# The inverse roots of a head pair's vector lengths: worked out on 88 rows of 12 columns, moved there and back by DMA

## What is computed

```python
def l2_normalize(x):
    xf = x.astype(jnp.float32)
    return xf * lax.rsqrt(jnp.sum(jnp.square(xf), axis=-1, keepdims=True) + EPS)

q = l2_normalize(q.reshape(bsz, t, GDN_HEADS, GDN_DK)) * (GDN_DK ** -0.5)
k = l2_normalize(k.reshape(bsz, t, GDN_HEADS, GDN_DK))
...
y = rms_norm(o, gdn_norm) * jax.nn.silu(zf)
```

## Time and profile before

| | |
|---|---|
| median of 3 runs | 1422.48 us (1421.45 to 1423.62) |
| the profiled execution | 1424.37 us, of which its span is 1422.6 us |
| busy: PE, DVE, ACT | 98%, 71%, 60% of the span |
| mean granted TensorE clock | 0.992 |
| DMA | 180 MB, 127 GB/s on the mean |

### The profile page before, as it was taken

How to read it: one execution, slowest core, us unless ns; L and a number is a source line. 1 busy time by engine, 2 the same in 40 slices (tenths; PEclk the granted TensorE clock), 3 DMA queues, 4 the chain that set the end, 5 groups by cost and what they waited for, 6 DMA issues and landing times.

```text
span 1422.6 us, 30023 instructions
## 1 busy us (share of the span) xinstructions
PE 1387.7 (98%) x9428; PEld 1172.2 (82%) x9428; DVE 1015.9 (71%) x3674; ACT 858.1 (60%) x2780; POOL 290.1 (20%) x339
## 2 busy tenths in 40 slices
PE   9999999999999999999999999999999999999998
PEld 7877887877778777778677787778778999999998
DVE  5767667787777787878778777878665667777543
ACT  5445688686666776666865667666784453444332
POOL 3012222222322222322322312222241000000000
PEclk9999999999999999999999999999999999999999
DMA  9443327644456443375444473434644565555551
GB/s 279 125 118 58 85 50 149 164 104 74 94 119 150 112 107 76 82 170 119 90 98 91 110 141 83 79 76 111 172 91 161 163 238 175 179 178 177 177 179 60
DMA packets 282890, 180.05 MB, mean 127 GB/s; under 512 B 183072, under 2 KB 229696, under 8 KB 282728
## 3 DMA queue, kind: packets, MB, share of 16 engines
q1 hardware_dynamic: 282418, 177.86, 49.4%
q10 hardware_dynamic: 318, 0.33, 0.1%
HBM read 134.32 MB, written 6.77 MB: 99 GB/s over the span
## 4 chain that ended last, share of the span: by engine, by line
PE 81%; DVE 8%; ACT 6%; issue 2%; SPq 1%; DMA 1%; POOL 0%; DVEq 0%; ACTq 0%
PE ps L2067 13%; PE ps L2069 12%; PE ps L2068 12%; PE ps L2471 6%; PE ps L2472 6%; PE ps L2473 6%; ACT ksq L895 2%; PE ps L2142 2%; PE ps L2089 2%; PE ps L2419 2%; PE ps L2143 2%; PE ps L2144 2%; PE ps L2420 2%; PE ps L2421 2%; PE ps L1951 2%
## 5 line engine op out<-in xcount | busy, mean ns | idle before, releaser
L2067 PE MATMUL ps<-ukh,cTh 128*128 128x512 f32 x1024 | 418.1, 408 | 5.5 <-DVE sparts L1285 4.6
L895 ACT ACTIVATE ksq<-ps 128x128 f32<-128x128 f32 x1024 | 268.2, 277 | 252.2 <-PE ps L2069 251.6
L2068 PE MATMUL ps<-ukl,cTh 128*128 128x512 f32 x1024 | 402.6, 393 | 0.0
L2069 PE MATMUL ps<-ukh,cTl 128*128 128x512 f32 x1024 | 402.5, 393 | 0.0
L1285 DVE CUSTOM_DVE_ANT_0 prod<-ps,qb 128x128 f32<-128x128 f32 x1024 | 234.5, 286 | 27.6 <-ACT ksq L895 23.3
L2067 PEld LDWEIGHTS ps<-ukh,cTh 128*128 128x128 f32 x1024 | 194.4, 190 | 60.0 <-issue 22.6
L2069 PEld LDWEIGHTS ps<-ukh,cTl 128*128 128x128 f32 x1024 | 193.9, 189 | 43.0
L2068 PEld LDWEIGHTS ps<-ukl,cTh 128*128 128x128 f32 x1024 | 194.4, 190 | 34.4
L747 POOL TENSOR_TENSOR rk<-kss,mhalf 128x8 f32<-128x8 f32 x128 | 218.4, 1706 | 10.6
L895 ACT ACTIVATION_READ_ACCUMULATOR ksq<-ps 128x1 f32 x1024 | 212.4, 208 | 0.0
L882 ACT ACTIVATE cTr<-turned 128x1024 uint16<-128x1024 uint16 x126 | 174.7, 1386 | 2.7 <-DMA turned<-planes 2.7
(11 more groups left out here) (504 smaller groups left out, 2702.1 us busy)
## 6 DMA issues: line engine op xcount, KB each, us to landing
clat<-cache_mla SPq DMA_DIRECT2D x128, 256.0 KB, 2.6
wraw<-w_in SPq DMA_DIRECT2D x16, 1024.0 KB, 5.2
wraw<-w_up SPq DMA_DIRECT2D x16, 1024.0 KB, 5.4
wraw<-w_down SPq DMA_DIRECT2D x16, 1024.0 KB, 5.0
braw<-w_in SPq DMA_DIRECT2D x24, 512.0 KB, 4.5
crope<-cache_mla SPq DMA_DIRECT2D x128, 32.0 KB, 2.4
qb<-scratch SPq DMA_DIRECT2D x16, 256.0 KB, 3.7
sst<-state_gdn SPq DMA_DIRECT2D x32, 128.0 KB, 3.5
```

What stands on the lines that cost most here:

```text
L895: i = nc.scalar.activation(ksq[m % 3], ps[:, k % 3, P * h:P * h + P], ACT.Square, accum_out=kss[:, n // 4 % 2, n % 4, h0 + h:h0 + h + 1]). ...
L2067: mm(out, cTh[:, n % 2, c], ukh[:, c, cols], start=c == 0, stop=False)
L2068: mm(out, cTh[:, n % 2, c], ukl[:, c, cols], start=False, stop=False)
L2069: i = mm(out, cTl[:, n % 2, c], ukh[:, c, cols], start=False, stop=c == 3)
```

## The change

- The sums of squares of a pair's four rows go to four rows of one group instead of four groups of 32 (L2166: one accumulation over shifted windows of a constant, `start` at the first and `stop` at the last), and DVE reads 4 rows of 264. In the same way the outputs' two rows.
- SP lays each of these rows out on 22 rows of 12 columns (`compact`: one DMA in SBUF for each row, four for the lengths, two for the outputs). Root, reciprocal and Newton step then work on 88 (or 44) rows of 12 columns, in the tile `lc`; the split is gone. The constant column that holds the queries' factor has it on the first 44 rows instead of 64.
- SP writes the result to DRAM (`roots_out`), waits for it, and reads it back on all 128 partitions (`roots_back`, 4 x 264 or 2 x 264 columns). The products that spread the rows (24 calls of `spread_row` in all, with two products each) are gone. DVE scales two heads with one instruction, from SBUF.
- `STEPS`: after step 16 come `ROOT`, `ROOT_OUT`, `ROOT_BACK` and one empty slot before 17; steps 45 and 46 are gone. A pair has 50 slots. The outputs' Newton step, transfers and scaling are done in slots 0, 1, 2 and 14 of the next pair (slot 5 after the last pair), and the first two loads of the next phase, `z_load(0)` and `z_load(1)`, move from slot 232 to slot 241.
- ACT's root of the lengths moves from step 15 to the end of step 16, behind a wait for the four `compact` DMAs, and that of the outputs from step 43 to 44, behind a wait for two.

```diff
-ROOT = 47
-STEPS = list(range(14)) + [None, 14, 15, 16, ROOT] + list(range(17, 47))
+ROOT, ROOT_OUT, ROOT_BACK = 47, 48, 49
+STEPS = list(range(14)) + [None, 14, 15, 16, ROOT, ROOT_OUT, ROOT_BACK, None] + list(range(17, 45))
...
+def tail_slot(i):
+
+    b, p = divmod(i - B_START, B_SLOTS)
+    return (b - 1, p) if 1 <= b <= HP else (None, None)
+
+
+def scale_slot(b):
+    return 14 if b + 1 < HP else 5
...
+            def compact(name, n_):
+                sp.wait_ge(S("a_read"), a_count(name))
+                for c in range(n_):
+                    sp.dma_start(lc[22 * c:22 * c + 22, 0, :], lr[c:c + 1, :].rearrange("c (a b) -> c a b", b=12)).then_inc(S("compacted"), 16)
+
+            def roots_out(b, c0, n_):
+                sp.wait_ge(S("root_ready"), 2 * b + 1 + c0 // 4)
+                sp.dma_start(lengths[b, c0:c0 + n_, :].rearrange("c (a b) -> (c a) b", b=12), lc[0:22 * n_, 3, :]).then_inc(S("roots_landed"), 16)
+
+            def roots_back(b, c0, n_, rows_, sem):
+                sp.wait_ge(S("roots_landed"), 16 * (2 * b + 1 + c0 // 4))
+                sp.dma_start(rows_[:], lengths[b:b + 1, c0:c0 + n_, :].to_broadcast([P, n_, T])).then_inc(S(sem), 16)
+
+            def tail_loads(b, p):
+                if p == 1:
+                    roots_out(b, 4, 2)
+                if p == 2:
+                    roots_back(b, 4, 2, orows, "orows_landed")
+
             def pair_loads(b, k):
+                if k == 15:
+                    compact(f"l2r_{b}", 4)
+                if k == ROOT_OUT:
+                    roots_out(b, 0, 4)
+                if k == ROOT_BACK:
+                    roots_back(b, 0, 4, hrows, "hrows_landed")
...
                 if k == 43:
+                    compact(f"osr_{b}", 2)
                     sp.wait_ge(S("a_read"), a_count(f"out3_{b}"))
...
-                if i == B_START + HP * B_SLOTS + 1:
+                if i == B_START + HP * B_SLOTS + scale_slot(HP - 1) + 1:
+                    sp.wait_ge(S("out_scaled"), HP)
                     z_load(0)
                     z_load(1)
...
-                if k == 15:
-                    act.wait_ge(S("a_read"), a_count(f"l2r_{b}"))
-                    nc.scalar.activation(lr[:, 1], lr[:, 0], ACT.Sqrt).then_inc(S("row_sqrt"), 1)
                 if k == 16:
...
                     i.then_inc(S("b_read"), 1)
+                    act.wait_ge(S("compacted"), 16 * (6 * b + 4))
+                    nc.scalar.activation(lc[:, 1], lc[:, 0], ACT.Sqrt).then_inc(S("row_sqrt"), 1)
...
-                if k == 43:
-                    act.wait_ge(S("a_read"), a_count(f"osr_{b}"))
-                    nc.scalar.activation(lr[0:64, 1], lr[0:64, 0], ACT.Sqrt).then_inc(S("row_sqrt"), 1)
+                if k == 44:
+                    act.wait_ge(S("compacted"), 16 * (6 * b + 6))
+                    nc.scalar.activation(lc[0:44, 1], lc[0:44, 0], ACT.Sqrt).then_inc(S("row_sqrt"), 1)
...
-            def newton_start(rows_, count):
+            def newton(rows_, count, scale):
                 v.wait_ge(S("row_sqrt"), count)
...
-                x, y, t_ = lr[0:rows_, 0], lr[0:rows_, 1], lt3[0:rows_]
+                x, y, t_, r_ = lc[0:rows_, 0], lc[0:rows_, 1], lc[0:rows_, 2], lc[0:rows_, 3]
+                link(V.reciprocal(y, y))
                 link(V.tensor_tensor(t_, y, y, ALU.mult))
                 link(V.tensor_tensor(t_, t_, x, ALU.mult))
                 link(V.tensor_scalar(t_, t_, -0.5, 1.5, ALU.mult, ALU.add))
-                link(V.scalar_tensor_tensor(x, y, scale, t_, ALU.mult, ALU.mult))
-                split(x, lrh[0:rows_], lrl[0:rows_], sem)
+                V.scalar_tensor_tensor(r_, y, scale, t_, ALU.mult, ALU.mult).then_inc(S("root_ready"), 1)
...
                 if k in (17, 18):
-                    for c in range(2 * (k - 17), 2 * (k - 17) + 2):
-                        V.tensor_tensor(qkv[:, c, :], qkv[:, c, :], bank(f"lb{c}")[:, 0:T], ALU.mult).then_inc(S("a_read"), 1)
+                    v.wait_ge(S("hrows_landed"), 16 * b + 16)
+                    cs = slice(2 * (k - 17), 2 * (k - 17) + 2)
+                    V.tensor_tensor(qkv[:, cs, :], qkv[:, cs, :], hrows[:, cs, :], ALU.mult).then_inc(S("heads_scaled"), 1)
...
+            def tail_dve(b, p):
+                if p == 0:
+                    newton(44, 2 * b + 2, 1.0)
+                if p == scale_slot(b):
+                    v.wait_ge(S("orows_landed"), 16 * b + 16)
+                    heads = slice(2 * b, 2 * b + 2)
+                    V.scalar_tensor_tensor(oT[:, heads, :], oT[:, heads, :], par[:, PR_GDN:PR_GDN + 1], orows[:], ALU.mult, ALU.mult).then_inc(S("out_scaled"), 1)
...
                     for c in range(4):
-                        i = mm(p_[32 * c:32 * c + 32, 0:T], window(0, 32), lsq[:, c, :], start=True, stop=True)
+                        i = mm(p_[0:32, 0:T], window(c, 32), lsq[:, c, :], start=c == 0, stop=c == 3)
...
-                if k in (17, 18):
-                    pe.wait_ge(S("row_rstd"), 2 * b + 1)
-                    for c in range(2 * (k - 17), 2 * (k - 17) + 2):
-                        spread_row(f"lb{c}_{b}", P, 32 * c, lrh[:], lrl[:])
...
-                if k == 46:
-                    pe.wait_ge(S("row_rstd"), 2 * b + 2)
-                    for hh in range(2):
-                        spread_row(f"ob{hh}_{b}", P, 32 * hh, lrh[:], lrl[:])
```

More of the change, by code:

```diff
@@ L304, in build @@
         assert e <= C_NEG.stop * 4
-        lrl, e = place("lrl", [P, T], F32R, taken["krT"][0] + 4 * T)
-        lr, e = place("lr", [P, 2, T], F32, taken["krT"][0])
+        lr, e = place("lr", [4, T], F32, taken["krT"][0])
+        lc, e = place("lc", [88, 4, 12], F32, e)
         assert e <= taken["decay_raw"][1]
@@ L367, in build @@
         sm, o = place("sm", [P, 8, 2 * NS], F32, o)
-        lrh, _ = place("lrh", [P, T], F32R, o)
-        lt3, o = place("lt3", [P, T], F32, o)
+        orows, _ = place("orows", [P, 2, T], F32, taken["lT"][0])
+        assert taken["orows"][1] <= taken["kd"][1]
         EARLY = o
@@ L372, in build @@
         lsq, _ = place("lsq", [P, 4, T], F32, EARLY)
+        hrows, _ = place("hrows", [P, 4, T], F32, EARLY)
         scrow, _ = place("scrow", [24, 6, P], F32, e)
@@ L416, in build @@
         assert o <= ATT
+        lengths = nc.dram_tensor("lengths", (HP, 6, T), F32, kind="Internal").ap()
         ps = ctx.enter_context(nc.psum_tensor("ps", [P, 8, 512], F32))
@@ L640, in _ @@
                 b, k = pair_slot(i)
+                tb, tp = tail_slot(i)
+                if tb is not None:
+                    tail_loads(tb, tp)
                 if b is not None:
                     pair_loads(b, k)
-                if i == B_START + HP * B_SLOTS + 1:
+                if i == B_START + HP * B_SLOTS + scale_slot(HP - 1) + 1:
+                    sp.wait_ge(S("out_scaled"), HP)
                     z_load(0)
@@ L1699, in beside @@
             def beside(i):
+                tb, tp = tail_slot(i)
+                if tb is not None:
+                    tail_dve(tb, tp)
                 b, k = pair_slot(i)
@@ L2175, in pair_pe @@
                     b_done(i)
[L2176 to L2179 removed]
                 if k == 19:
[L2181 removed]
+                    pe.wait_ge(S("heads_scaled"), 2 * b + 2)
                     four("qk", 4, lambda out, w: mm(out, chunk(2, w), chunk(0, w), start=True, stop=True))
@@ L2290, in pair_pe @@
                     for hh in range(2):
-                        i = mm(p_[32 * hh:32 * hh + 32, 0:T], window(0, 32), osq[:, hh, :], start=True, stop=True)
+                        i = mm(p_[0:32, 0:T], window(hh, 32), osq[:, hh, :], start=hh == 0, stop=hh == 1)
                     a_done(i)
-                if k == 46:
-                    pe.wait_ge(S("row_rstd"), 2 * b + 2)
-                    for hh in range(2):
-                        spread_row(f"ob{hh}_{b}", P, 32 * hh, lrh[:], lrl[:])
             def front_pe(i):
```

30 lines of the change are left out of this document (10 added, 20 removed).

## The result

The changed kernel takes 1409.6 us (median of four executions, 1407.8 to 1410.3) against 1422.0 us of the kernel before in the same session: 0.9916 of it, 95% interval 0.990 to 0.993. The forecast was 1410.

What follows compares the result with a forecast made beforehand. PE, busy for 98% of the span, was taken as the bound. 1424.4 - 22.1 (waits, clock) + 1.2 (PE's work) + 3.2 (ACT) + 5.3 (new waits) = 1412.0 us, 1410 for the median; range 1400 to 1423.

Steps and rivals of the forecast that it cites:

- Waits removed: PE's waits at the eight root computations, 12.8 us, and two for DVE's scores, 1.5 and 0.8, go: 15.1 us less.
- The falls of the clock: PE's drops to 1.2 GHz after four of the eight roots go with the waits: 7.0 us less.
- one fall at 1.8: Among the new waits, one new fall of PE's clock was added: 1.8 us, between none and three falls.
- PE's work: Spreading products go, 5.8 us less; sums of squares run in series, 7.0 us more; net 1.2 us more on the path.
- DVE (28 us less): DVE's eight roots, on 12 columns, take 3.5 us less each, 28 us, none of it on the path by itself.
- (a): Slot 51, pair 0's four compacting copies land late behind page loads: 1.5 us on PE, between 0 and 3.
- (b): Slot 83, two copies for pair 0's outputs land late behind page loads: 1.0 us on PE, between 0 and 4.
- (c): Slot 155, pair 2's read lands late behind page loads: 1.0 us on PE, between 0 and 3.
- What is late next: With PE's waits gone PE would wait for ACT: 0.8 us comes back for each pair, 3.2 us.
- Slower by SP's queue: Rival: SP held 2.6 us by each of eight store round trips makes later turns late; median 1433 us, chance 0.14.
- signs of being wrong: PE waits for scores or low part above 10 us, DVE's planes waiting much longer on turns, or four clock falls.
- The fixed cost of a transfer: A small copy was priced at 3.1 us from issue to landing; the skill's 2.0 us would give near 1408.

Runs made afterwards that it cites:

- e4: Kernel before the change, PE's spreading kept, with reciprocal and Newton step on 12 of the 264 columns: 1411.9 us, 0.994 of the kernel before.
- e5: Changed kernel with unread work added so that DVE is as busy at each root as before the change: 1415.1 us, 0.994 of the kernel before.
- e3: Changed kernel with the sums of squares in groups of 32 rows side by side, as before the change: 1403.4 us, 0.988 of the kernel before.
- e11: Changed kernel with 48 unread products added on PE, as many as the removed spreading had: 1412.0 us, 0.993 of the kernel before.
- e7: Changed kernel with all DMAs of the roots issued by POOL instead of SP: 1430.6 us, 1.0045 of the kernel before.
- e1: Changed kernel with the next pair's load of scrow issued ahead of the compacting copies and the sst stores: 1403.4 us, 0.987 of the kernel before.
- e2: Changed kernel with the read of the four rows issued ahead of its slot's page loads and turn: 1405.9 us, 0.989 of the kernel before.
- e8: Changed kernel with the edits of e1, e2 and e3 together: 1399.7 us, 0.984 of the kernel before.
- e9: Kernel of e8 with the eight sst stores moved from step 43 to step 44: 1395.5 us, 0.982 of the kernel before.
- e10: Kernel of e9 with the roots' DMAs after the first page load of a slot, and the outputs' read one slot later: 1395.9 us, 0.981.
- e6: Changed kernel with SP writing each set of roots to DRAM twice and waiting for both: 1415.6 us, 0.994 of the kernel before.
- e12: Changed kernel, unedited, measured again in five executions: 1408.9 us, 0.990 of the kernel before.

## Why the prediction was right, point by point

- **Waits removed (15.1 us).** Right, and there was more. PE's idle time in the stretch was 20.0 us before; beside the 12.8 of the earlier trace rows and the two of the earlier trace rows, 3.3 us were waits for the low part of the pair's weights (`bwl`), which DVE makes. They are gone after, and not because DVE has less to do: e4 keeps them and e5 has none, so the new slots of pairs 1 and 3 took them away. I had read only the waits that the change names, and not asked what the renumbering would do to the others.
- **The falls of the clock (7.0 us back, one new at 1.8).** Half right. All old ones went, but new ones of 5.0 us came, so 2.0 us was saved, not 5.2. The step that failed is that of one fall at 1.8: two new stalls, of 2.64 and 3.19 us, were each as long as those that had cost a fall in the kernel before (1.84 and 3.22 us), and one of the two falls cost 3.4.
- **PE's work (+1.2 us).** Its two halves were nearly right: the sums in series measured 6.4 (e3) for the 7.0 put, the products 6.8 of busy time (e11) for the 5.8. Together that is -0.4 and not +1.2. The two windows have the same sign and more of it: 3.55 us less busy time, 2.0 of it the clock, 1.5 left. The 1.1 us between the two readings are not explained.
- **DVE (28 us less).** 25.5 us (1015.9 to 990.4 us busy), and the reciprocal took 0.23 us.
- **(a) and (b), the compacting copies behind page loads.** In size at the low end of the ranges, 0 for the 2.5 us put, and the waits of ACT that were to show them are not there: in this profile ACT never waits for a copy, and PE's idle time from 300 to 320 us is 0.12. Two things in the working were off. I had ACT at its root 8 to 12 us after the turn of slot 50; it was there after 14.2 us (302.10 to 316.30). And I had priced a copy at 3.1 us by the earlier trace rows; e7 shows 1.8. The last copy's issue ended at 314.79 us, so SP was as late as forecast, and with the shorter landing that was soon enough.
- **(b) once more.** There was a loss at slot 83, but not in the copies: `scrow`, 2.64 us and 3.4 of clock, 6.0 in all and the largest term that came back. The prediction said that every instruction that is moved counts, and then only followed those of the roots. Step 44 had lost the two slots behind it, and step 43's stores had landed on page loads, by nothing but the renumbering of `STEPS`. e1 put it at 6.2 us.
- **(c), the read of pair 2.** The place was right (slot 155, DVE waiting in slot 157 alone), the size was not: 3.19 us on PE and 1.6 of clock for the 1.0 put. e2 shows that the read ahead of the page loads makes the page and the next turn late instead.
- **What is late next (ACT, 3.2 us).** Wrong for this kernel. PE's idle time after the roots did not come back: 300 to 340 us has 0.12 us of it. Only with the sums side by side (e3, e8, e9, e10) does a wait for scores of 0.9 to 2.0 us stand behind pair 0's root, at 317 to 319 us; whether ACT is behind it no run shows. Where PE waits now, the chain goes over SP's late turn or page to DVE's scores.
- **Slower by SP's queue (0.14).** SP's queue was the right one to look at, but not at the place that this rival named. Behind the stores' round trips SP waited 7.1 us in all, not 8 x 2.6 = 20.8, and e6 prices such holding: 5.9 of 17 us reach the end. The mean wait of the earlier trace rows was a fair cover there. It failed where page loads share the slot, which the prediction had under (a), (b) and (c). One of its signs of being wrong did come up: DVE's planes waited 23.5 us for turns after 13.2 before.
- **The fixed cost of a transfer.** The Trainium skill (DMA: Bandwidth & Descriptors, "Anatomy of one DMA") put it at about 2.0 us where my row had 3.1. From POOL's queue (e7) the copies of 1.0 KB took 1.8 us and the stores of 4.1 KB 1.9, so there the trace agrees with the page; the stores of 2.1 KB took 3.0, and of those it doesn't. Its warning on small descriptors ("Why small descriptors are slow") is not tested here: all these stores go in pieces of 48 bytes, and no run stores the same bytes in larger ones.

That the time came out within 1 us of the forecast is luck: errors of both signs met, single ones of up to 6 us. What the prediction had right is the direction and its main cause, PE no longer waiting for the roots. Against the prediction's -12.4 us the stretch changed by -13.7. Saved beyond it: 4.9 us of old waits (20.0 for 15.1), 2.7 of PE's work (-1.5 for +1.2), 3.2 for ACT, 2.5 for (a) and (b), 1.8 for the fall without a place, 15.1 in all. Lost beyond it: 6.0 at slot 83, 3.8 at (c) (3.19 + 1.6 for 1.0), and 4.1 in waits of at most 1.6 us that I had put nowhere (9.9 - 2.64 - 3.19), 13.9 in all. The difference, 1.2 us, is what is seen.

## What to carry to other kernels

When steps of a schedule written out by hand are inserted or removed, list every transfer in the slots behind them, with its distance to its use and with what shares its slot, also those that the change doesn't mention: here one such load cost 6 us beside a gain of 12, and mending it and the burst around it gave 9 to 10 (6.2 in e1, 2.8 to 4.2 from e8 to e9). A transfer queue has to be read by its longest burst between two urgent items (here 12.0 us from the first page load to the turn, 417.80 to 429.80), not by its mean wait. Renumbering can also give: 3.3 us of waits went when two pairs of heads moved from even to odd slots. And an engine's idle share says nothing about its queue as long as one instruction can hold it for 15 us.

## What was not expected of the hardware

- A single cross-partition maximum on POOL held its queue for 14.7 us (e7, 306.36 to 321.07), with 0.6 us of it shown as busy, and as long in the kernel before (307.61 to 322.31).
- A fall of TensorE's clock is not in proportion to the stall ahead of it: 2.64 us cost 3.4 us, 3.19 us cost 1.6 (both in one execution), while 1.59 us at 1032 us cost nothing, and in e2 3.3 us in two pieces cost nothing either. Nor does the place decide: in e12, the same kernel, the wait for `scrow` was longer (3.66 us) and cost half as much (1.7), and the 3.01 us at 718 cost 3.4. Read in windows of 1 us, every fall in the stretch of these traces costs either 1.7 or 3.4 us.
- Eight small products side by side in four groups of 32 rows took 0.63 us, the same eight in one group 1.94, and the difference was there in the time of the whole, 6.2 us over four pairs.
